# An fp32 transformer kernel on one core: another order of products in a pair of panels, and ScalarE's follow-up work an entry later

## The chip, the core and the metric

The kernel runs on one core of a Trainium2 chip. It is written instruction by instruction, with one program for each engine and semaphores between them: TensorE (PE, matmul), VectorE (DVE), ScalarE (ACT), GpSimd (POOL) and SyncE (SP, which only starts loads). The metric is the device time of one execution in microseconds (us).

## What is computed

Two transformer blocks over 256 tokens of width 2048, in fp32. Cut to what matters here:

```
# block 1
proj = rmsnorm(x) @ w_in ; da = diff_attention(...) ; ret = retention(...) * silu(rg)
x = x + concat(da, ret) @ w_o
hx = rmsnorm(x) ; hm = rmsnorm(mem)
xq, xk, xv = hx @ w_xq, hm @ w_xk, hm @ w_xv
x = x + attention(xq, xk, xv) @ w_xo
hf = rmsnorm(x)
x = rmsnorm(x + (silu(hf @ w_gate) * (hf @ w_up)) @ w_down)
# block 2
h = rmsnorm(x) * (1 + scale) + shift          # shift, scale, gate = silu(c) @ w_ada + b_ada
q, k, v, gate_a, u, gate_p = split(h @ w_in_2)
y_a = windowed_gqa(q, k, v) * silu(gate_a) ; y_p = multiscale_pool(u) * silu(gate_p)
g_a, g_p = split(sigmoid(h @ w_merge + b_merge))
merged = g_a * (y_a @ w_branch_attn) + g_p * (y_p @ w_branch_pool)
out = x + gate * rmsnorm(merged @ w_out)
```

Nearly all of the arithmetic is the product of 256 tokens with weight matrices, and all weights are read once.

## The kernel before

**Splitting.** PE multiplies fp32r operands, which carry fewer bits than fp32. So each operand is split into a high and a low part, and each product becomes three matmuls: high by high, low by high, high by low (the lines L1015, L1016, L1017; `ah`, `al`, `bh`, `bl`, `fah` and so on are the activations' parts, `whi` and `wlo` those of the weights).

**Halves and entries.** The weights come as halves of 256 rows by 512 columns (512 KB, one DMA each, in 8 slots `raw`). A *panel* is 512 output columns over all rows: 4 chunks of two halves for most, its two token tiles of 128 tokens (tile 0 and tile 1) in two PSUM banks `ps`. For each *entry* of the stream (840 of them) ACT makes the high part `whi` (L1524) and DVE the low part `wlo` (L2222, high part subtracted from `raw`), into one of 4 buffers; PE then takes the entry in one *step*. A normal step is 12 matmuls (both tiles). While PE is at step k, ACT and DVE may make entry k+3, and that of k+4 only when step k is done.

**Pairs.** 40 pairs of panels (q0 to q39; a first panel f and a second panel s) save work by Strassen's scheme in the Winograd form on their first chunk: seven *products* M1 to M7 of one tile and six matmuls each, in place of eight. Their weights are the four halves of the first chunks or sums of them; their activations are the plain forms or combined ones (`fah`, `fal`, `fbh`, `fbl`). M5, M6, M7 and M4 take sums of halves: DVE makes such a sum in the raw slot (L2238), and it waits there for its own conversion before (it overwrites what that read). The dictionary `sums_before` says ahead of which entry's conversion each sum is made. A product's result has to reach up to two banks: ACT copies a bank to `side` (L1122, `snapshot`: s5 of M5, s1 of M1, s3 of M7; the bank belongs to the other panel until then), and DVE makes the difference "v" (L1647, `difference`), for which M7 waits. The order of a pair with 4 chunks before is M3, M5, n1, M1, M2, n2, M6, n3, n4, M7, n5, M4, n6, ..., where n1, n2, ... are normal entries of f, counted as entries 0 to 12: n1 is entry 2, M1 is 3, M2 is 4, M6 is 6, n3 is 7, M7 is 9, M4 is 11. In this numbering snapshot s5 is taken at n1's step, whose tile 1 needs M5's bank back, s1 at M2's, the difference at n3's, s3 at n5's.

**What follows a panel.** When a panel ends, each engine runs a `begin(p)` for its kind: `o`, `xo`, `d`, `e`, `m` are added to X or to a tensor (`residual`, L1724; `merge_gate`, DVE L2054 and ACT L1396), `g`, `rg`, `ga`, `gp` get a sigmoid on ACT (L1174) and a product on DVE (`gate_product`), `u` is DVE's `up` (L1926 and L1929). ACT squares X for the norms (`square`, L1046; `residual_squares`). Where that work is a generator, `jobs.start` puts it in a queue of which one piece is run in each step; `aside.start` puts it in a second queue, whose next piece is run in each step, right after that step's `make`, the conversion of one more entry. A plain call in `begin` runs at once, ahead of the next conversion. The second panel of a pair has its tile-1 result whole in its PSUM bank and its tile-0 result split over bank and `side`, so DVE adds both first (`summed`, L1625).

**Names used here.** The kinds of panels in order: v, tq, rg (block 1's w_in), o, xk, xv, xq, xo, then g, u (gate, up) and d, e (down, the last down panels), then block 2's q, ga, pu, gp, kv, m (merge), ba, bp, w_out. q6 is o2/o3, q7 xk0/xk1, q14 xo2/xo3, q15 g0/u0, q16 g1/u1, q33 pu0/gp0. The residual of a pair's second panel is taken at the start of the pair behind it.

## Time and profile before

| | |
|---|---|
| median of 3 runs | 2186.24 us (2186.16 to 2189.12) |
| the profiled execution | 2193.24 us, its span 2191.4 us |
| PE busy | 2095.8 us, 96% of the span |
| DVE busy | 1681.4 us, 77% |
| ACT busy | 1172.8 us, 54% |
| granted clock of PE, mean | 0.989 of full |
| moved by DMA | 453.75 MB, 207 GB/s |

Busy PE is an upper bound on useful PE: matmuls are pipelined, and the profile models their ends. A main matmul lasts 390 ns by the profile but the next starts 0.227 us after it where nothing holds it, so what the profile calls idle is about 0.17 us less than the gap that a wait makes from start to start. Times of one place come from one execution, the profiled one.

### The profile page before, as it was taken

How to read it: one execution, taken by the hardware profiler on the slowest of the kernel's cores; microseconds unless marked ns; L12 is line 12 of the kernel's file. 1: busy time of each engine (PE TensorE's matmuls, PEld its weight loads, DVE VectorE, ACT ScalarE, POOL GpSimd, SP SyncE). 2: the span in 40 equal slices, each digit the busy share in tenths (PEclk: the TensorE clock that was granted, in tenths of full speed). 3: DMA queues.
4: the chain of work that ended last, by engine and by line, in shares of the span. 5: the costliest groups of instructions: out<-in, count | busy, mean ns of one | idle time of the engine just before them, and what ended most of it. 6: DMA issues, size and time to landing. Idle time of an engine off the chain costs nothing.

```text
span 2191.4 us, 25376 instructions
## 1 busy us (share of the span) xinstructions
PE 2095.8 (96%) x9334; PEld 1707.6 (78%) x9334; DVE 1681.4 (77%) x1839; ACT 1172.8 (54%) x1519; POOL 72.1 (3%) x94
## 2 busy tenths in 40 slices
PE   9999999899999999999999999999899999899998
PEld 7877787688887777787778877887677787678786
DVE  6767777776765678888888888887687767788875
ACT  6555555655554565554455544555655554554453
POOL 1000000000000000000000000000400000000000
PEclk9999999999999999999999999999999999999999
DMA  9444546466444447676567766665455556669653
GB/s 329 154 154 168 171 165 223 161 213 220 154 154 154 154 154 277 242 275 247 211 221 255 279 224 225 237 250 189 141 189 173 173 183 216 225 227 356 230 203 108
DMA packets 218955, 453.75 MB, mean 207 GB/s; under 512 B 14400, under 2 KB 16592, under 8 KB 218704
## 3 DMA queue, kind: packets, MB, share of 16 engines
q1 hardware_dynamic: 212928, 432.07, 56.0%
q0 software_dynamic: 5616, 19.94, 2.7%
q8 instruction: 74, 1.21, 0.2%
q14 instruction: 49, 0.40, 0.1%
q10 hardware_dynamic: 288, 0.13, 0.0%
HBM read 447.88 MB, written 4.19 MB: 206 GB/s over the span
## 4 chain that ended last, share of the span: by engine, by line
PE 52%; DVE 20%; issue 11%; DMA 11%; ACT 6%; SPq 0%; POOL 0%; DVEq 0%; ACTq 0%; POOLq 0%
PE ps L1015 16%; PE ps L1017 15%; PE ps L1016 15%; DVE wlo L2222 9%; DMA raw<-in_w_up_dram 3%; ACT whi L1524 3%; DVE raw L2238 3%; DMA raw<-in_w_down_dram 3%; PE ps L607 1%; DMA raw<-in_w_gate_dram 1%; DMA raw<-in_w_o_dram 1%; DVE FR L1889 1%; DMA raw<-in_w_merge_dram 1%; DMA raw<-in_w_in_dram 1%; DVE FR L1625 1%
## 5 line engine op out<-in xcount | busy, mean ns | idle before, releaser
L2222 DVE TENSOR_TENSOR wlo<-raw,whi 128x1024 fp32r<-128x1024 f32 x832 | 1005.7, 1221 | 323.6 <-ACT whi L1524 318.0
L1524 ACT ACTIVATE whi<-raw 128x1024 fp32r<-128x1024 f32 x840 | 880.0, 1056 | 624.4 <-PE ps L1017 372.1
L1015 PE MATMUL ps<-whi,ah 128*128 128x512 f32 x1618 | 650.6, 402 | 33.2 <-ACT side L1122 17.2
L1017 PE MATMUL ps<-whi,al 128*128 128x512 f32 x1618 | 634.3, 392 | 0.0
L1016 PE MATMUL ps<-wlo,ah 128*128 128x512 f32 x1618 | 633.9, 392 | 0.0
L1015 PEld LDWEIGHTS ps<-whi,ah 128*128 128x128 f32 x1618 | 306.1, 189 | 108.7 <-ACT side L1122 21.0
L1015 PE MATMUL ps<-whi,bh 128*128 128x512 f32 x862 | 345.8, 401 | 18.5 <-ACT side L1122 12.4
L1017 PEld LDWEIGHTS ps<-whi,al 128*128 128x128 f32 x1618 | 306.0, 189 | 66.1
L1016 PEld LDWEIGHTS ps<-wlo,ah 128*128 128x128 f32 x1618 | 306.5, 189 | 60.5 <-issue 0.2
L1017 PE MATMUL ps<-whi,bl 128*128 128x512 f32 x862 | 338.2, 392 | 0.0
L1016 PE MATMUL ps<-wlo,bh 128*128 128x512 f32 x862 | 337.9, 392 | 0.0
L2238 DVE TENSOR_TENSOR raw<-raw 128x1024 f32<-128x1024 f32 x160 | 195.9, 1224 | 45.3 <-DVE wlo L2222 24.2
L1015 PEld LDWEIGHTS ps<-whi,bh 128*128 128x128 f32 x862 | 163.5, 190 | 58.4 <-ACT side L1122 14.3
L1017 PEld LDWEIGHTS ps<-whi,bl 128*128 128x128 f32 x862 | 163.1, 189 | 35.1
L1016 PEld LDWEIGHTS ps<-wlo,bh 128*128 128x128 f32 x862 | 163.5, 190 | 33.2 <-issue 1.0
L1889 DVE SCALAR_TENSOR_TENSOR FR<-raw,Z,FR 128x1024 f32<-128x1024 f32 x90 | 111.5, 1279 | 0.9 <-DMA raw<-in_w_ada_dram 0.9
L1015 PE MATMUL ps<-whi,fah 128*128 128x512 f32 x208 | 85.0, 408 | 9.0 <-DVE wlo L2222 4.2
L1122 ACT ACTIVATE side<-ps 128x512 f32<-128x512 f32 x120 | 71.1, 592 | 32.1 <-PE ps L1017 31.9
L1017 PE MATMUL ps<-whi,fal 128*128 128x512 f32 x208 | 81.9, 394 | 0.0
L1016 PE MATMUL ps<-wlo,fah 128*128 128x512 f32 x208 | 81.6, 392 | 0.0
L2280 POOL TENSOR_TENSOR Z<-Z 128x2 f32<-128x2 f32 (+1 forms) x18 | 11.7, 655 | 1556.9 <-DVE Z L1570 854.2
L1625 DVE TENSOR_TENSOR FR<-ps,side 128x512 f32<-128x512 f32 x81 | 53.3, 686 | 8.5 <-PE ps L1017 8.3
(235 smaller groups left out, 1346.3 us busy)
## 6 DMA issues: line engine op xcount, KB each, us to landing
raw<-in_w_in_dram SPq DMA_DIRECT2D x168, 512.0 KB, 5.6
raw<-in_w_ada_dram SPq DMA_DIRECT2D x96, 512.0 KB, 8.0
raw<-in_w_gate_dram SPq DMA_DIRECT2D x88, 512.0 KB, 7.6
raw<-in_w_up_dram SPq DMA_DIRECT2D x88, 512.0 KB, 6.5
raw<-in_w_down_dram SPq DMA_DIRECT2D x88, 512.0 KB, 7.7
raw<-in_w_merge_dram SPq DMA_DIRECT2D x64, 512.0 KB, 6.6
raw<-in_w_o_dram SPq DMA_DIRECT2D x32, 512.0 KB, 8.0
raw<-in_w_xk_dram SPq DMA_DIRECT2D x32, 512.0 KB, 6.3
```

The lines of the kernel that those rows point to most:

```text
L607: ins = e.transpose(T[b].ap[:, kk * 256 + t * 128:kk * 256 + t * 128 + 128], src[:, t, (2 * b + kk) * 128:(2 * b + kk + 1) * 128], ident[: ...
L1015: e.matmul(o, xh[:, k, tokens], wh, start=first, stop=False, skip_group_check=more)
L1016: e.matmul(o, xh[:, k, tokens], wl, start=False, stop=False, skip_group_check=more)
L1017: ins = e.matmul(o, xl[:, k, tokens], wh, start=False, skip_group_check=more, stop=kk == 1 and (st.end or st.form in READ))
L1122: done(e.activation(side_of(pair[place[0]], place[1]), bank_of(pair[panel], t)[:, :], ACT.Copy), "snap")
L1524: done(e.activation(whi[:, n % HALVES, :], raw[:, item % RAWS, :], ACT.Copy), "hi")
L1625: return e.tensor_tensor(dst, src, side_of(p, t), side_op(p))
L1889: done(e.scalar_tensor_tensor(acc, src, csilu[:, k:k + 1], acc, ALU.mult, ALU.add), "ada")
L2222: done(e.tensor_tensor(wlo[:, n % HALVES, :], src, whi[:, n % HALVES, :].bitcast(F32), ALU.subtract), "lo")
L2238: done(e.tensor_tensor(place(item), place(add), place(item), ALU.subtract if minus else ALU.add), "t_sum")
L2280: e.tensor_tensor(dst, src, mhalf[:, 0:n], ALU.pow).then_inc(s["r"], 1)
```

## The change

In a pair of 4 chunks the order becomes M3, M5, n1, M1, n2, M6, M2, n3, n4, M7, ...: n2 is entry 4, M6 is 5, M2 is 6. Snapshot s1 is taken at n2's step, the difference v at M2's (entry 6). DVE makes M6's sum ahead of entry 1's conversion instead of entry 2's, M7's ahead of entry 5's instead of 4's. A pair of 3 chunks keeps its order of entries. On ACT the squares behind `o` and `xo` panels, the merge gates and the squares of the last down panels go through `aside`, and so run one conversion later; on DVE the means that need the squares do. For second panels DVE's additions and gate products and ACT's sigmoids of gates take tile 1 first; the merge gates' sigmoids on ACT still take tile 0 first. In `up` tile 1's product comes first, then the sum of tile 0 and its product, with nothing between these two.

ACT behind the end of panel o3, that is in the first steps of q7. `sq2` are the squares of the X of o3, `ev10` and `ev11` DVE's additions of o panels' results, `pre` the matmul side of a snapshot; before:

```order
L1524 ACTIVATE whi<-raw 128x1024 [waits s_half,s_raw4]
L1258 ACTIVATE bh<-FR,G 128x256 [waits s_half,s_mt_t2]
L1258 ACTIVATE bh<-FR,G 128x256 x3
L1046 ACTIVATE junk,Z<-X 128x512 [waits s_sq2,s_ev11,s_ev10]
L1046 ACTIVATE junk,Z<-X 128x512 [waits s_sq2]
L1524 ACTIVATE whi<-raw 128x1024 [waits s_half,s_raw2]
L1524 ACTIVATE whi<-raw 128x1024 [waits s_half,s_raw3]
L1122 ACTIVATE side<-ps 128x512 [waits s_pre,s_half]
L1524 ACTIVATE whi<-raw 128x1024 [waits s_half,s_raw5]
```

and in the changed kernel:

```order
L1535 ACTIVATE whi<-raw 128x1024 [waits s_half,s_raw4]
L1267 ACTIVATE bh<-FR,G 128x256 [waits s_half,s_mt_t2]
L1267 ACTIVATE bh<-FR,G 128x256 x3
L1535 ACTIVATE whi<-raw 128x1024 [waits s_half,s_raw2]
L1054 ACTIVATE junk,Z<-X 128x512 [waits s_sq2,s_ev11,s_ev10]
L1054 ACTIVATE junk,Z<-X 128x512 [waits s_sq2]
L1535 ACTIVATE whi<-raw 128x1024 [waits s_half,s_raw5]
L1130 ACTIVATE side<-ps 128x512 [waits s_pre,s_half]
L1535 ACTIVATE whi<-raw 128x1024 [waits s_half,s_t_sum]
```

The two squares (L1046, now L1054) have moved behind the conversion that followed them, and one conversion instead of two lies between them and the snapshot (L1122, now L1130).

DVE from M5's sum of pair q16 on, with the `up` of u0 in it (L2238 are sums, L2222 conversions, L1625 the sum of tile 0, L1926 and L1929 the products); before:

```order
L2238 TENSOR_TENSOR raw<-raw 128x1024 [waits s_lo,s_t_sum,s_raw6,s_raw5]
L2222 TENSOR_TENSOR wlo<-raw,whi 128x1024 [waits s_hi] x2
L2238 TENSOR_TENSOR raw<-raw 128x1024 [waits s_lo,s_t_sum,s_raw5,s_raw4]
L2222 TENSOR_TENSOR wlo<-raw,whi 128x1024 [waits s_hi]
L1625 TENSOR_TENSOR FR<-ps,side 128x512 [waits s_snap,s_half]
L1926 SCALAR_TENSOR_TENSOR FR<-ps,Z,FR 128x512 [waits s_gated]
L1929 SCALAR_TENSOR_TENSOR FR<-FR,Z 128x512 [waits s_ev10]
L2222 TENSOR_TENSOR wlo<-raw,whi 128x1024 [waits s_hi]
L2238 TENSOR_TENSOR raw<-raw 128x1024 [waits s_lo,s_t_sum,s_raw4,s_raw6]
L2222 TENSOR_TENSOR wlo<-raw,whi 128x1024 [waits s_hi] x3
L2238 TENSOR_TENSOR raw<-raw 128x1024 [waits s_lo,s_t_sum,s_raw4,s_raw7]
L2222 TENSOR_TENSOR wlo<-raw,whi 128x1024 [waits s_hi]
```

and in the changed kernel (L2257, L2241, L1643, L1944 and L1948 in this order):

```order
L2257 TENSOR_TENSOR raw<-raw 128x1024 [waits s_lo,s_t_sum,s_raw6,s_raw5]
L2241 TENSOR_TENSOR wlo<-raw,whi 128x1024 [waits s_hi]
L2257 TENSOR_TENSOR raw<-raw 128x1024 [waits s_lo,s_t_sum,s_raw5,s_raw4]
L2241 TENSOR_TENSOR wlo<-raw,whi 128x1024 [waits s_hi] x2
L1944 SCALAR_TENSOR_TENSOR FR<-ps,Z,FR 128x512 [waits s_gated,s_half]
L1643 TENSOR_TENSOR FR<-ps,side 128x512 [waits s_snap,s_half]
L1948 SCALAR_TENSOR_TENSOR FR<-FR,Z 128x512 [waits s_ev10]
L2241 TENSOR_TENSOR wlo<-raw,whi 128x1024 [waits s_hi] x2
L2257 TENSOR_TENSOR raw<-raw 128x1024 [waits s_lo,s_t_sum,s_raw4,s_raw6]
L2241 TENSOR_TENSOR wlo<-raw,whi 128x1024 [waits s_hi] x2
L2257 TENSOR_TENSOR raw<-raw 128x1024 [waits s_lo,s_t_sum,s_raw4,s_raw7]
L2241 TENSOR_TENSOR wlo<-raw,whi 128x1024 [waits s_hi]
```

M6's sum (the second L2238) is one conversion earlier, M7's (the third) one later; the product of tile 1 stands ahead of the sum of tile 0.

DVE further on in the same pair, up to the difference for M7 (L1647, now L1665); before:

```order
L1616 TENSOR_TENSOR FR<-FR 128x2x128 [waits s_dve]
L2222 TENSOR_TENSOR wlo<-raw,whi 128x1024 [waits s_hi]
L1620 TENSOR_TENSOR fbl<-FR,fbh 128x1024 [waits s_f_hi]
L2222 TENSOR_TENSOR wlo<-raw,whi 128x1024 [waits s_hi]
L1647 TENSOR_TENSOR side<-ps,side 128x512 [waits s_snap,s_half]
L2222 TENSOR_TENSOR wlo<-raw,whi 128x1024 [waits s_hi] x5
```

and in the changed kernel:

```order
L1634 TENSOR_TENSOR FR<-FR 128x2x128 [waits s_dve]
L2241 TENSOR_TENSOR wlo<-raw,whi 128x1024 [waits s_hi]
L1665 TENSOR_TENSOR side<-ps,side 128x512 [waits s_snap,s_half]
L1638 TENSOR_TENSOR fbl<-FR,fbh 128x1024 [waits s_f_hi]
L2241 TENSOR_TENSOR wlo<-raw,whi 128x1024 [waits s_hi] x6
```

The difference now stands ahead of the low part of the combined form (L1620, now L1638) and of one more conversion.

The diff (without the empty parts of its context):

```diff
--- before.py
+++ after.py
@@ -334,13 +334,16 @@
         product("M5", b12, b11, start=True, job=False)
         normal(f, *next(todo), snap=("s5", q))
         product("M1", b11, start=True, job=False)
-        product("M2", b21, start=True, snap=("s1", q))
         if chunks == 4:
+            normal(f, *next(todo), snap=("s1", q))
+            product("M6", b22, b12)
+            product("M2", b21, start=True, snap=("v", q))
             normal(f, *next(todo))
-        product("M6", b22, b12)
-        normal(f, *next(todo), snap=("v", q))
-        if chunks == 4:
             normal(f, *next(todo))
+        else:
+            product("M2", b21, start=True, snap=("s1", q))
+            product("M6", b22, b12)
+            normal(f, *next(todo), snap=("v", q))
         product("M7", b11, b22, minus=True)
         normal(f, *next(todo), snap=("s3", q))
         product("M4", b21, b22, aside=q)
@@ -446,6 +449,11 @@
 
         def side_op(p):
             return ALU.add if role[p][0] else ALU.subtract
+
+        def by_bank(p):
+
+
+            return (1, 0) if role.get(p, (0, 0))[0] else (0, 1)
 
         def nth_of(kinds, paired):
 
@@ -1165,7 +1173,7 @@
                         e.wait_ge(*gate_done(gate_before(p), t))
                 if root is not None:
                     e.wait_ge(s["r"], root_n(root))
-                for t in range(2):
+                for t in by_bank(p):
                     by = 1.0 if root is None else root_col[root][:, t:t + 1]
                     src = bank_of(p, t)[:, :]
                     if side_of(p, t) is not None:
@@ -1249,6 +1257,7 @@
                 wait_panel(p)
                 for t in range(2):
                     square(X[:, t, j * PW:(j + 1) * PW], ss[:, 2 * j + t:2 * j + t + 1], name)
+                yield
 
             def split_mem(j):
                 hi, _ = hi_lo(("mem", j))
@@ -1297,12 +1306,13 @@
 
             def down2(p, j):
                 for t in range(2):
-                    c = 4 * t + j
-                    xs = X[:, t, j * PW:(j + 1) * PW]
                     e.wait_ge(*ev(p, t))
-                    square(xs, ssf[:, c:c + 1], "sqf")
+                    square(X[:, t, j * PW:(j + 1) * PW], ssf[:, 4 * t + j:4 * t + j + 1], "sqf")
+                yield
+                for t in range(2):
                     e.wait_ge(s["gf_x"], 2 * j + t + 1)
-                    square(xs, ssg[:, c:c + 1], "sqg")
+                    square(X[:, t, j * PW:(j + 1) * PW], ssg[:, 4 * t + j:4 * t + j + 1], "sqg")
+                yield
 
             def scale_chunk(j, t):
                 e.wait_ge(s["r"], root_n(f"rr{t}"))
@@ -1394,6 +1404,7 @@
                 for t in range(2):
                     e.wait_ge(*ev(p, t))
                     done(e.activation(SIG[i][:, t, :], SIG[i][:, t, :], ACT.Sigmoid), "mg_sig")
+                yield
 
             def turn_merged(n):
                 yield
@@ -1437,7 +1448,7 @@
                     aside.start(sigmoids(p, GR, SG, "x"))
                     jobs.start(ret_pair(i))
                 elif kind == "o":
-                    residual_squares(p, i, ss_2, "sq2")
+                    aside.start(residual_squares(p, i, ss_2, "sq2"))
                     if i < 3:
                         jobs.start(turn_x(f"hx{i}", ("hx", i), gcols("nx", i)))
                     if i == 0:
@@ -1453,7 +1464,7 @@
                     if i == 0:
                         jobs.start(make_forms("xo"))
                 elif kind == "xo":
-                    residual_squares(p, i, ss_3, "sq3")
+                    aside.start(residual_squares(p, i, ss_3, "sq3"))
                     jobs.start(turn_x(f"hf{i}", ("hf", i), gcols("nffn", i)))
                     if i == 0:
                         jobs.start(make_forms("hf"))
@@ -1466,7 +1477,7 @@
                     if i % 4 == 0:
                         jobs.start(make_forms(f"h{i}"))
                 elif kind == "e" and i < 3:
-                    down2(p, i)
+                    aside.start(down2(p, i))
                 elif kind == "e":
                     last_down(p, t)
                 elif kind == "kv":
@@ -1481,7 +1492,7 @@
                     aside.start(sigmoids(p, GS[i], SG3, None))
                     jobs.start(pool_job(i))
                 elif kind == "m":
-                    merge_gate(p, i)
+                    aside.start(merge_gate(p, i))
                 elif kind == "ba" and i == 2:
                     jobs.start(pause(4))
                 elif kind == "bp":
@@ -1569,6 +1580,13 @@
                     after_own(done(e.tensor_reduce(src, given, AX_X, ALU.add)))
                 done(e.tensor_scalar(col, src, 1.0 / total, EPS, ALU.mult, ALU.add), "ms")
 
+            def mean_of(name, squares, ss):
+
+                yield
+                e.wait_ge(s[squares], 8)
+                mean(name, sums[name], 2, D, by_tile(ss))
+                yield
+
             def by_tile(ss):
                 return ss.rearrange("p (j t) -> p t j", t=2)
 
@@ -1696,7 +1714,7 @@
                 aside.start(gate_product(p, dst, sg, root))
 
             def gate_product(p, dst, sg, root):
-                for t in range(2):
+                for t in by_bank(p):
                     count["sig"] += 1
                     e.wait_ge(s["sig"], count["sig"])
                     src = bank_of(p, t)[:, :]
@@ -1719,7 +1737,7 @@
                 wait_sum(p, 1)
                 if p in role:
                     e.wait_ge(*side_taken(p, 1 - role[p][0]))
-                for t in range(2):
+                for t in by_bank(p):
                     xs = X[:, t, j * PW:(j + 1) * PW]
                     took(e.tensor_tensor(xs, bank_of(p, t)[:, :], xs, ALU.add), p, t)
 
@@ -1921,20 +1939,22 @@
                     yield
 
             def up(p, i):
-                summed(p, 0, HH[:, 0, :])
+                wait_sum(p, 1)
                 wait_gate(index["g", i], 0, 1)
                 took(e.scalar_tensor_tensor(HH[:, 1, :], bank_of(p, 1)[:, :], root_col["r3"][:, 1:2], ZG[:, 1, :],
                                             ALU.mult, ALU.mult), p, 1)
+                summed(p, 0, HH[:, 0, :])
                 e.wait_ge(*ev(p, 0))
                 done(e.scalar_tensor_tensor(HH[:, 0, :], HH[:, 0, :], root_col["r3"][:, 0:1], ZG[:, 0, :], ALU.mult,
                                             ALU.mult), "hh")
 
             def down2(p, j):
-                residual(p, j)
+                yield
                 for t in range(2):
                     xs = X[:, t, j * PW:(j + 1) * PW]
                     e.wait_ge(s["sqf"], 2 * j + t + 1)
                     done(e.tensor_tensor(xs, xs, GF[:, j * PW:(j + 1) * PW], ALU.mult), "gf_x")
+                yield
 
             def scale_chunk(j, t):
                 e.wait_ge(s["r"], root_n(f"rr{t}"))
@@ -2049,7 +2069,7 @@
             def merge_gate(p, i):
                 wait_sum(p, 1)
                 e.wait_ge(*side_taken(p, 1 - role[p][0]))
-                for t in range(2):
+                for t in by_bank(p):
                     also = BB[i] if side_of(p, t) is None else SIG[i][:, t, :]
                     took(e.tensor_tensor(SIG[i][:, t, :], bank_of(p, t)[:, :], also, ALU.add), p, t)
 
@@ -2117,8 +2137,7 @@
                 elif kind == "o":
                     residual(p, i)
                     if i == 3:
-                        e.wait_ge(s["sq2"], 8)
-                        mean("r2", sums["r2"], 2, D, by_tile(ss_2))
+                        aside.start(mean_of("r2", "sq2", ss_2))
                     else:
                         jobs.start(to_stationary(f"hx{i}", ("hx", i), gcols("nx", i)))
                     if i == 0:
@@ -2136,8 +2155,7 @@
                 elif kind == "xo":
                     residual(p, i)
                     if i == 3:
-                        e.wait_ge(s["sq3"], 8)
-                        mean("r3", sums["r3"], 2, D, by_tile(ss_3))
+                        aside.start(mean_of("r3", "sq3", ss_3))
                     jobs.start(to_stationary(f"hf{i}", ("hf", i), gcols("nffn", i)))
                     if i == 0:
                         jobs.start(make_forms("hf"))
@@ -2155,7 +2173,8 @@
                 elif kind == "e" and i < 3:
                     if i == 0:
                         e.wait_ge(s["norm_f"], 16)
-                    down2(p, i)
+                    residual(p, i)
+                    aside.start(down2(p, i))
                 elif kind == "e":
                     last_down(p, t)
                 elif kind == "kv":
@@ -2240,7 +2259,8 @@
 
             sums_before = {}
             for _, at in stream.pairs:
-                sums_before |= {at["M3"]: at["M5"], at["M5"] + 1: at["M6"], at["M2"]: at["M7"], at["M6"] + 1: at["M4"]}
+                sums_before |= {at["M3"]: at["M5"], at["M5"]: at["M6"], at["M1"] + 2: at["M7"],
+                                max(at["M2"], at["M6"]) + 1: at["M4"]}
 
             done(e.memset(tbl[:, :], 0.0), "tbl_zero")
             e.wait_ge(s["tbl_zero"], 1)
```

A `yield` ends a piece of such work; the next piece runs in the next step.

## Rows read from the trace of the kernel before

**Rows 1.** The page: busy time of the engines, and the chain that ended last

```profile
PE 2095.8 (96%) x9334; PEld 1707.6 (78%) x9334; DVE 1681.4 (77%) x1839; ACT 1172.8 (54%) x1519; POOL 72.1 (3%) x94
PE 52%; DVE 20%; issue 11%; DMA 11%; ACT 6%; SPq 0%; POOL 0%; DVEq 0%; ACTq 0%; POOLq 0%
```

**Rows 2.** Waits of PE: engine, tile, line, releaser: us in total, times, longest us

```profile
PE ps L1015 <- ACT side L1122: 29.6, 13, 5.0
PE ps L1015 <- DVE wlo L2222: 27.0, 31, 2.3
PE ps L1015 <- DVE side L1647: 7.3, 6, 1.9
```

**Rows 3.** Timeline of ACT, pair q14: start, duration, line, operation, [idle before <-releaser]

```profile
763.72 0.63 ACT L1046 ACTIVATE junk<-X 128x512 bf16<-128x512 f32 x1 [5.20 <-DVE X L1724]
765.10 1.99 ACT L1524 ACTIVATE whi<-raw 128x1024 fp32r<-128x1024 f32 x2
766.99 0.58 ACT L1122 ACTIVATE side<-ps 128x512 f32<-128x512 f32 x1
767.47 1.05 ACT L1524 ACTIVATE whi<-raw 128x1024 fp32r<-128x1024 f32 x1
```

**Rows 4.** Timeline of PE, the waits on s5 in q7, q14 and q15

```profile
417.38 0.79 PE L1015 MATMUL ps<-whi,bh 128*128 128x512 f32 x1 [5.01 <-ACT side L1122]
767.62 0.57 PE L1015 MATMUL ps<-whi,bh 128*128 128x512 f32 x1 [3.48 <-ACT side L1122]
814.93 0.50 PE L1015 MATMUL ps<-whi,ah 128*128 128x512 f32 x1 [1.24 <-ACT side L1122]
```

**Rows 5.** Timeline of DVE and PE, the merge gate of q36

```profile
1861.63 1.28 DVE L2054 TENSOR_TENSOR FR<-ps,FR 128x512 f32<-128x512 f32 x2
1866.01 0.50 PE L1015 MATMUL ps<-whi,ah 128*128 128x512 f32 x1 [2.58 <-ACT side L1122]
```

**Rows 6.** Timeline of ACT and PE, the gate of q33

```profile
1700.67 0.63 ACT L1174 ACTIVATE FR<-FR 128x512 f32<-128x512 f32 x1
1703.27 0.50 PE L1015 MATMUL ps<-whi,ah 128*128 128x512 f32 x1 [1.21 <-ACT side L1122]
```

**Rows 7.** Timeline of DVE in q16, and the page's group of its sums

```profile
853.76 2.44 DVE L2222 TENSOR_TENSOR wlo<-raw,whi 128x1024 fp32r<-128x1024 f32 x2
856.40 1.23 DVE L2238 TENSOR_TENSOR raw<-raw 128x1024 f32<-128x1024 f32 x1 [0.20 <-DVE wlo L2222]
874.32 1.23 DVE L1620 TENSOR_TENSOR fbl<-FR,fbh 128x1024 fp32r<-128x1024 f32 x1
L2238 DVE TENSOR_TENSOR raw<-raw 128x1024 f32<-128x1024 f32 x160 | 195.9, 1224 | 45.3 <-DVE wlo L2222 24.2
```

**Rows 8.** Timeline of PE, the waits on the difference in q7 and q16

```profile
436.27 0.47 PE L1015 MATMUL ps<-whi,fbh 128*128 128x512 f32 x1 [1.86 <-DVE side L1647]
877.43 0.47 PE L1015 MATMUL ps<-whi,fah 128*128 128x512 f32 x1 [1.36 <-DVE side L1647]
```

**Rows 9.** Stretches: us, busy time of PE, PEld, DVE, ACT, POOL, PEclk, DMA share, GB/s

```profile
437.00:440.50 3.50, 3.50 (x12) 2.77 (x12) 3.02 (x7) 2.15 (x5) 0.72 (x1) 0.54 0.41 102
1867.00:1870.40 3.40, 3.40 (x9) 2.64 (x9) 3.40 (x4) 1.06 (x1) 0.00 (x0) 0.50 0.00 0
1963.90:1967.40 3.50, 3.50 (x16) 2.85 (x17) 3.50 (x4) 2.37 (x4) 0.00 (x0) 1.00 0.03 9
1006.00:1036.00 30.00, 28.80 (x127) 23.19 (x125) 23.91 (x24) 11.49 (x12) 0.00 (x0) 1.00 0.91 334
```

**Rows 10.** Timeline of PE, waits on low parts in q16 (two), q20 and e2

```profile
858.81 0.50 PE L1015 MATMUL ps<-whi,ah 128*128 128x512 f32 x1 [0.77 <-DVE wlo L2222]
864.43 0.50 PE L1015 MATMUL ps<-whi,ah 128*128 128x512 f32 x1 [0.76 <-DVE wlo L2222]
1036.66 0.50 PE L1015 MATMUL ps<-whi,fbh 128*128 128x512 f32 x1 [1.86 <-DVE wlo L2222]
1547.65 0.50 PE L1015 MATMUL ps<-whi,bh 128*128 128x512 f32 x1 [0.73 <-DVE wlo L2222]
```

## The prediction, made before the changed kernel had run

> **What bounds the kernel now.** I read the page first: TensorE (PE) is busy 96% of the span, VectorE (DVE) 77%, and the chain that ended last is PE for 52% of the span and DVE for 20% [rows 1]. So what can be won is PE's idle time, and most of the chain's DVE part lies where DVE's preparation of a weight half reaches PE just in time. Then the waits of PE: three kinds stand out, and the change touches all three [rows 2]. (1) 29.6 us in 13 waits on ScalarE's (ACT) copy of M5's bank, the snapshot; by the kernel's order this is tile 1 of the first normal entry of a pair. (2) 27.0 us in 31 waits on a low part. (3) 7.3 us in 6 waits on the difference that M7 needs. The time of one such wait, its pair (q0 to q39, in the order of the program) and its entry come from PE's timeline, where I counted matmuls: a normal entry has twelve, a product six. My sum goes against the profiled execution's own time, 2193.24 us (span 2191.4); it is 7.0 above the median of the runs, 2186.24, so I take the gain off that median.
>
> **The change part by part.**
>
> *ACT work an entry later.* In the pair o2/o3, after the residual of the panel before, ACT stood idle 5.20 us for X, ran the two squares (763.72 to 765.10), two conversions of high parts (1.99 us), and only then the snapshot at 766.99 [rows 3]; PE stood 3.48 us for it [rows 4]. The change puts one of these two conversions ahead of the squares, into the idle time; the order shows it, one conversion left between the squares and the snapshot. The second of two conversions adds 1.99 − 1.05 = 0.94, say 0.95 us, to the first in these rows, so the snapshot comes 0.95 earlier. Nothing else holds it: M5 ended long before. This holds in four pairs, q6, q7, q14 and q15, whose waits are all longer than 0.95 (the last is 1.24 [rows 4]): −3.8. The cost, that squares come later, falls on DVE's mean of them, which is put off as well. What the whole wait holds beyond that stays, since the squares still block the queue ahead of the snapshot.
>
> *Merge gates (m panels, q36 to q38).* The same move: −0.95. But DVE now adds tile 1 first and ACT's sigmoid still asks for tile 0 first. DVE's two additions take 1.28 together [rows 5], so the second ends some 0.60 after the first, and the sigmoids start 0.60 later: −0.35 each, −1.05 for three waits of 2.58. *The sigmoid in q33* takes tile 1 from PSUM first, and no longer waits for DVE's sum ahead of it; one activation of 0.63 leaves the path of a wait of 1.21 [rows 6]: −0.65.
>
> *M7's wait.* The difference moves from the seventh step of a pair to the sixth, so DVE makes it ahead of one conversion (and, in the feed-forward panels, of the 1.23 us low part of the forms) instead of behind. That is 1.14 to 2.3 us earlier by the lengths of these operations [rows 7]. It covers q3's 0.3 and q7's 1.86 [rows 8]: −2.2. Behind q7's wait the clock granted to PE is 0.54 of full for 3.5 us [rows 9], that is 1.2 GHz in place of 2.4 for nearly all of it. It costs 3.5 × 0.46 = 1.6 us at most. If the wait is gone I take this window to be gone, less a little: −1.4. Against it: which waits bring such a window isn't plain from the rows. Behind q36's wait of 2.58, at 1866.01, there was one (0.50), behind q38's equally long one at 1963.75 none (1.00) [rows 5, 9].
>
> *Feed-forward pairs q16 to q29.* There DVE is just in time. M2's low part is late in nine pairs, 6.0 us together by PE's timeline, of which q16's 0.76 is typical [rows 10]; by start to start each is 0.17 more: 7.5. M7's difference is late in three, 1.36 in q16 [rows 8], 3.8 together, with 0.17 each 4.3. The change puts M7's sum behind the conversion of the half at entry 4, which frees a sum there: 1.14 + 0.20 of wait = 1.35, more than any of these stalls; M6's sum goes ahead of M5's low part. So 11.8 could go. Off it come three costs. First, the up panels: DVE multiplies tile 1 first, sums tile 0, and must then wait for its own result. Where DVE waits for itself now, ahead of a sum, it stands 0.20 us [rows 7]. 11 × 0.20 = 2.2. Second, M6's sum ahead of M5's low part: in q16 the conversion ran 853.76 to 856.20, PE took M5 at 856.5, a slack of 0.3, so M5 comes 1.35 − 0.3 = 1.05 late; but the first normal entry behind it already waited 0.77 (0.94 start to start) for the low part behind that sum [rows 7, 10], and that one doesn't move. Net +0.15, in eight pairs 1.2. Third, part of it comes back at the next pair's M3 in q20, q21, q26 and q27, whose first conversion hangs on loads that come in a burst (the DMA share is 0.91 over 30 us ahead of q20's wait of 1.86) [rows 9, 10]: 1.0. In all −11.8 + 2.2 + 1.2 + 1.0 = −7.4. The bounds: −11.8, and 0 if all comes back at M3.
>
> On the up panels a rule speaks against my cost. The Trainium skill, "VectorE: DVE Perf Modes", section "The DRAIN you can't avoid", says that eight copies with a semaphore after each take as long as eight with one at the end, the semaphore costs nothing extra. By it the self-waits are free and the sum would be 2.2 better. The trace doesn't agree: two operations of DVE without a wait between them overlap by 0.08 (the pair of conversions takes 2.44 for twice 1.22), those that wait for the one before start 0.20 after its end [rows 7]. I keep 2.2.
>
> *The rest.* q31's M2 0.5. Down panels e0 to e2 (the last ones, ahead of the final norm): the squares leave the way of the conversions behind them, whose lateness PE saw twice, 0.73 [rows 10] and 0.52 in the panel before: −1.25. M6 now stands ahead of M2, and its bank or side may wait for M1's snapshot where ACT is busy (q2, q32, q33): +0.6, between 0 and 3 × 0.58, a snapshot's length [rows 3]. Loads: halves are released in the order of the new entries, no more and no fewer; M2 and M6 swap two raw slots a microsecond or two: 0, hidden behind queues that run a pair ahead outside the feed-forward, and inside counted in the third cost.
>
> Sum: −3.8 − 1.05 − 0.65 − 2.2 − 1.4 − 7.4 − 0.5 − 1.25 + 0.6 = −17.65. The profiled execution would be 2175.6, the median 2168.6. I say 2169.
>
> **The rivals.**
> *A, the feed-forward gain is given back.* The stretch from a pair's last products to the next M3 is paced by loads (DMA share 0.91 [rows 9]); then what M2 and M7 win is waited for at M3 or the first normal entry. Against it: only four of 14 pairs have a wait at M3, and the burst is started by DVE's conversions, which come earlier too. The 7.4 and the e panels' 1.25 are gone: −9.0, 2177.
> *B, more low-clock windows go.* Waits of 3.48, 5.01, 3.48 and 2.58 [rows 4, 5] shrink to about 2.5, 4.1, 2.5 and 2.2. If q6, q14, q36 and q37 lose theirs, four times 1.5 come on top: −23.7, 2162.5. For it: the 2.58 at 1963.75 that went without a window; against it: the 2.58 at 1866.01 that didn't [rows 9].
> *C, slower: M6's sum ahead of M5's low part throws every feed-forward pair back.* The price is s per pair at M5, up to 1.35, if the wait of the first normal entry isn't relieved in turn. In 14 pairs 18.9 less the 2.3 relieved in q16, q21 and q26, plus the up panels' 2.2, against −9.25 for what lies outside these pairs: +9.6, 2196. It decides from s = (9.25 + 2.3 − 2.2)/14 = 0.67 on. Against it: in q16 the slack leaves 1.05 and 0.94 of it is relieved [rows 7, 10].
> *D, ACT's moves do nothing*, since the snapshot's start is set by X and not by what stands between. Then −4.85 and half the clock are missing: −12, 2174. This lies in the forecast's range.
>
> **How the numbers follow.** Forecast with D 0.56, A 0.20, B 0.17, C 0.07. The likeliest alone: 2164 to 2174. The range holds A and B, and leaves out C and the outer ends: 2158 (B with the feed-forward's 11.8 instead of 7.4) to 2181 (A without the clock, the merges and half of the squares). No change, within 0.2% (4.4 us, about what a measurement can tell here), needs A to lose the squares' part as well, or a mild C: 0.08. Slower by more: C's stronger half and what I haven't seen: 0.07. Faster 0.85.
>
> **What would show it.** The 13 waits on the snapshot fall from 29.6 to about 25; the six on the difference nearly vanish; in q16 the wait at entry 4 is gone, and one of about 1.0 stands at M5 in place of that at the first normal entry; ACT's idle ahead of the squares falls by 1 each; DVE's sum of tile 0 in the up panels is followed by 0.20 of waiting. Sigmoids of q36 to q38 start 0.6 later than X's first addition ends. I am wrong if waits at M3 grow by as much as those at M2 shrink (A), if new waits at M5 are not matched by vanished ones (C), or if waits appear at M6 for M1's snapshot in more than three pairs.

## The result, and the profile after

| | before | changed |
|---|---|---|
| median of the runs | 2187.68 us (4 runs, 2186.16 to 2189.51) | 2174.6 us (4 runs, 2171.12 to 2177.47) |
| ratio of the runs | | 0.9939, 95% interval 0.992 to 0.9958 |
| the profiled execution | 2193.24 us | 2175.93 us |
| its span, mean granted clock | 2191.4 us, 0.989 | 2174.1 us, 0.993 |

The changed kernel is 13.1 us faster by the medians (0.6%), 17.3 us by the profiled executions. Forecast was 17.65 for both. The profiled execution came to 2175.93 us (2175.6 was forecast); the median, 2174.6, lies in the stated range of 2158 to 2181, 5.6 above the 2169 and just outside the likeliest stretch of 2164 to 2174. (One of the eleven executions of e2 below took 4645.87 us; its ratio leaves that one out, and its median is 2188.3 us without it and 2188.4 with it.) The page after, its busy times and the chain that ended last, against [rows 1]:

```profile
PE 2085.0 (96%) x9334; PEld 1700.7 (78%) x9334; DVE 1681.1 (77%) x1839; ACT 1173.4 (54%) x1519; POOL 74.2 (3%) x94
PE 57%; DVE 19%; issue 11%; DMA 8%; ACT 5%; POOL 0%; DVEq 0%; ACTq 0%; SPq 0%; POOLq 0%
```

No engine has less work; PE's busy time falls by 10.8 mostly because it runs less at the low clock. The waits of PE after, against [rows 2] (other lines between these are left out):

```profile
PE ps L1023 <- ACT side L1130: 24.6, 17, 4.0
PE ps L1023 <- DVE wlo L2241: 24.3, 29, 2.2
PE ps L756 <- DVE FR L1877: 1.5, 1, 1.5
PE ps L615 <- issue: 2.0, 2, 1.2
PE ps L788 <- DVE Z L1917: 2.1, 1, 2.1
PE ps L1023 <- DVE side L1665: 1.5, 1, 1.5
```

The snapshot's waits have lost 5.0 us but there are 17 instead of 13. The 13 that were there alone fell by 8.2, to 21.4; four new ones (M6 in q2, q32 and q33, M4 in q7) hold 3.2. Those on the difference fell from 7.3 to 1.5; those on low parts from 27.0 to 24.3 only; and three kinds have come (L615, L756, L788) that are PE's own jobs: its transposes and small products between the steps. (A job's piece is run behind a step, and PE waits there for what other engines make of the piece before.)

**Where the time lies.** I cut all traces at the start of each pair's M3. The granted clock falls to 0.5 of full (1.2 GHz instead of 2.4) in single stretches, most of them 3.4 us long, called low windows here. PE takes twice as long for the same work in one, so of each pair's length I took off half of the time at a granted clock of 0.5 within it (47.8 us in all before, 29.7 after). What is left, less that of the kernel before, in us:

| pairs | changed | e1 | e2 | e3 | f3 | f4 |
|---|---|---|---|---|---|---|
| q0 to q5 | +1.2 | +0.6 | +1.2 | −1.4 | −1.6 | −1.7 |
| q6, q7, q14, q15 | −3.8 | −5.8 | +0.8 | −6.9 | −12.1 | −12.5 |
| q12, q13 | +1.9 | −1.8 | +1.8 | +0.4 | +0.6 | +0.6 |
| q16 to q29 (feed-forward) | −4.7 | +2.5 | −6.3 | −4.8 | −4.2 | −5.5 |
| q30 and the e panels | −0.6 | −1.4 | −0.4 | −0.6 | −0.6 | −0.6 |
| q31 to q34 | +1.0 | −0.8 | +1.5 | +2.4 | +2.4 | +2.3 |
| q35 to q38 (merges) | −1.5 | −1.2 | −0.1 | −3.5 | −3.8 | −9.0 |
| rest | −1.8 | −1.8 | −0.5 | −0.9 | +0.3 | −0.3 |
| all | −8.3 | −9.6 | −2.0 | −15.3 | −19.0 | −26.7 |
| at the low clock, us | 29.7 | 35.9 | 51.5 | 25.4 | 16.6 | 11.5 |

(The columns are the experiments below, each from its one profiled execution; the rest holds the start, q8 to q11 and q39. A group repeats within about 1.5 us where nothing was changed, or 2 where a low window falls into a stretch with waits: the −1.8 of e1 at q12 is such a one.) So of the 17.35 us between the spans 8.3 are work and waiting, 9.05 are low-clock time. This split is not exact: before, q20 and q27 held one low window each, and in e1, which has the same order there, both went without a window and took as long (46.17 and 44.18 us, before 45.81 and 44.17). There PE waits for loads and low parts anyway, so these two windows cost nothing. Put so, work is −11.7 and the clock −5.6. Nor is all of the clock's part the change's doing. Besides the windows of q20 and q27, that behind q7's M7, half of the long one behind q7's snapshot and those of q36 and q37 went, 6.8 us in time together. Windows also went ahead of q0, in q1 and in q30, and others came in q2, q12 and q38; these six cancel, and a longer stretch in q39 costs 1.15. The window ahead of q0, where none of the moved work runs, is there in some of the versions and not in others. And the kernel before is here by its profiled execution, 5.6 us above its median, so a part of the differences in the traces isn't in the medians.

**ScalarE in q14**, to be read against [rows 3] (start, duration, line, operation, idle before it):

```profile
757.87 1.06 ACT L1535 ACTIVATE whi<-raw 128x1024 fp32r<-128x1024 f32 x1 [1.66 <-PE ps L1025]
760.97 0.63 ACT L1054 ACTIVATE junk<-X 128x512 bf16<-128x512 f32 x1 [2.04 <-DVE X L1742]
762.36 1.04 ACT L1535 ACTIVATE whi<-raw 128x1024 fp32r<-128x1024 f32 x1
763.30 0.57 ACT L1130 ACTIVATE side<-ps 128x512 f32<-128x512 f32 x1
```

The conversion at 757.87 now stands in the idle time ahead of the squares (5.20 has become 1.66 + 2.04), and the snapshot starts 2.33 us after the start of the squares, where it was 3.27: 0.94 earlier, as worked out. PE's waits on it in q7, q14 and q15, against [rows 4]:

```profile
412.91 0.50 PE L1023 MATMUL ps<-whi,bh 128*128 128x512 f32 x1 [4.01 <-ACT side L1130]
763.93 0.50 PE L1023 MATMUL ps<-whi,bh 128*128 128x512 f32 x1 [2.08 <-ACT side L1130]
810.21 0.50 PE L1023 MATMUL ps<-whi,ah 128*128 128x512 f32 x1 [0.24 <-ACT side L1130]
```

They were 5.01, 3.48 and 1.24: −1.00, −1.40, −1.00; q6's went from 3.48 to 2.46. At the start of the same entry PE's wait for the low part fell too, in q7 from 2.27 to 1.14 and in q6 from 0.66 to 0.23.

**VectorE and PE in q16**, against [rows 7, 10]; first DVE from M6's sum on, then PE at M5:

```profile
850.43 1.22 DVE L2257 TENSOR_TENSOR raw<-raw 128x1024 f32<-128x1024 f32 x1 [0.20 <-DVE wlo L2241]
851.58 2.35 DVE L2241 TENSOR_TENSOR wlo<-raw,whi 128x1024 fp32r<-128x1024 f32 x2
853.85 0.74 DVE L1944 SCALAR_TENSOR_TENSOR FR<-ps,Z,FR 128x512 f32<-128x512 f32 x1
854.51 0.68 DVE L1643 TENSOR_TENSOR FR<-ps,side 128x512 f32<-128x512 f32 x1
855.22 0.75 DVE L1948 SCALAR_TENSOR_TENSOR FR<-FR,Z 128x512 f32<-128x512 f32 x1
855.89 2.35 DVE L2241 TENSOR_TENSOR wlo<-raw,whi 128x1024 fp32r<-128x1024 f32 x2
```

```profile
852.85 0.50 PE L1023 MATMUL ps<-whi,fah 128*128 128x512 f32 x1 [0.90 <-DVE wlo L2241]
```

The sum stands ahead of M5's conversion, PE waits 0.90 (1.07 start to start) at M5, the first normal entry waits no more, and neither does M2. In `up` the third operation starts 0.71 after the second, where it was 0.66 before: the self-wait costs 0.05 here, and the three together 0.12, not 0.20.

**PE's own jobs in q4**: the transposes (L615) of what comes of the products L715 to L717. After:

```profile
269.20 0.59 PE L717 MATMUL ps<-FR 128*128 128x256 f32 x2
273.74 0.63 PE L615 MATMUL ps<-ident,FR 128*128 128x128 f32 x4 [1.18 <-issue]
```

and before:

```profile
271.15 0.59 PE L709 MATMUL ps<-FR 128*128 128x256 f32 x2
275.71 0.61 PE L607 MATMUL ps<-ident,FR 128*128 128x128 f32 x4
```

The distance is the same (4.54 and 4.56): it is what ACT, GpSimd and DVE need in between (squares, a root, a product). Before, PE had n2 and M6 to do in between, 2.72 and 1.36 us (12 and 6 matmuls at 0.227); now it has M6 and M2, twice 1.36, and stands 1.18 us. In q13 it is the same with a single step: the piece that waits was behind n2 and is now behind M6. Before, then after:

```profile
723.43 0.55 PE L748 MATMUL ps<-ident,FR 128*128 128x128 f32 x3 [0.17 <-DVE FR L1859]
```

```profile
721.10 0.66 PE L756 MATMUL ps<-ident,FR 128*128 128x128 f32 x4 [1.52 <-DVE FR L1877]
```

The piece ahead of it starts 6.51 us earlier in both traces (716.92 and 714.59).

### The profile page after: what moved, and what is told of

The parts are those of the page before. It is cut to its first block, busy times and chain, and to the rows that moved or that the text cites. A ratio compares the mean times of both kernels' runs of the same rounds, so it can differ in the third digit from the quotient of the medians.

```text
span 2174.1 us, 25372 instructions
## 1 busy us (share of the span) xinstructions
PE 2085.0 (96%) x9334; PEld 1700.7 (78%) x9334; DVE 1681.1 (77%) x1839; ACT 1173.4 (54%) x1519; POOL 74.2 (3%) x94
## 3 DMA queue, kind: packets, MB, share of 16 engines
q8 instruction: 74, 1.21, 0.2%
## 4 chain that ended last, share of the span: by engine, by line
PE 57%; DVE 19%; issue 11%; DMA 8%; ACT 5%; POOL 0%; DVEq 0%; ACTq 0%; SPq 0%; POOLq 0%
PE ps L1023 17%; PE ps L1025 17%; PE ps L1024 17%; DVE wlo L2241 8%; DVE raw L2257 3%; DMA raw<-in_w_down_dram 3%; DMA raw<-in_w_up_dram 2%; ACT whi L1535 2%; PE ps L615 1%; DMA raw<-in_w_merge_dram 1%; DMA raw<-in_w_o_dram 1%; DVE FR L1907 1%; DVE FR L1643 1%; DMA raw<-in_w_gate_dram 1%; PE ps L746 1%
## 5 line engine op out<-in xcount | busy, mean ns | idle before, releaser
L2241 DVE TENSOR_TENSOR wlo<-raw,whi 128x1024 fp32r<-128x1024 f32 x832 | 1005.4, 1221 | 307.0 <-ACT whi L1535 300.7
L2257 DVE TENSOR_TENSOR raw<-raw 128x1024 f32<-128x1024 f32 x160 | 195.9, 1225 | 47.2 <-DVE wlo L2241 25.2
L1130 ACT ACTIVATE side<-ps 128x512 f32<-128x512 f32 x120 | 71.1, 592 | 29.9 <-PE ps L1025 29.9
L1023 PEld LDWEIGHTS ps<-whi,fah 128*128 128x128 f32 x208 | 39.1, 188 | 32.7 <-DVE wlo L2241 20.4
```

The lines of the kernel that those rows point to most:

```text
L1023: e.matmul(o, xh[:, k, tokens], wh, start=first, stop=False, skip_group_check=more)
L1130: done(e.activation(side_of(pair[place[0]], place[1]), bank_of(pair[panel], t)[:, :], ACT.Copy), "snap")
L2241: done(e.tensor_tensor(wlo[:, n % HALVES, :], src, whi[:, n % HALVES, :].bitcast(F32), ALU.subtract), "lo")
L2257: done(e.tensor_tensor(place(item), place(add), place(item), ALU.subtract if minus else ALU.add), "t_sum")
```

## The experiments

Each kernel ran beside the kernel before on the same chip. The times are medians, the ratios go against the kernel before. The changed kernel, the e's, the f's and the g's stand in four groups, on different chips, beside which the kernel before had medians of 2187.68, 2188.8, 2190.41 and 2188.34 us: a difference of two medians across groups is uncertain by some 2 us.

**e1: the follow-up work alone.** The changed kernel with the lines of `_pair` and `sums_before` as they were:

```diff
-            normal(f, *next(todo), snap=("s1", q))
-            product("M6", b22, b12)
-            product("M2", b21, start=True, snap=("v", q))
+        product("M2", b21, start=True, snap=("s1", q))
+        ...
-                sums_before |= {at["M3"]: at["M5"], at["M5"]: at["M6"], at["M1"] + 2: at["M7"],
+                sums_before |= {at["M3"]: at["M5"], at["M5"] + 1: at["M6"], at["M2"]: at["M7"], at["M6"] + 1: at["M4"]}
```

> The follow-up work of the change (ACT through aside, tile 1 first, up's order, means put off) with the old order of the pair and the old places of the sums. My account of the two traces gives this half nearly all of the gain that does not hang on low-clock windows: the waits on the snapshot in q6, q7, q14, q15, q33 and q36 to q38 shrink as in the changed kernel, M5 and M6 get no new waits, PE's own jobs stay where they were. So about -9 us against the kernel before, 2178 to 2180. Rival (the order is the better half): -5 or less, and the new waits at M3 are there too.

Measured: 2178.31 us, ratio 0.9955 (0.9942 to 0.9967), before 2188.8. That is 10.5 us of the changed kernel's 13, and the intervals of the two ratios overlap. The waits of PE on the snapshot and the rest in its trace:

```profile
PE ps L1020 <- DVE wlo L2238: 27.6, 30, 1.7
PE ps L1020 <- ACT side L1127: 23.6, 13, 4.0
PE ps L1020 <- DVE side L1662: 6.8, 6, 1.5
```

13 waits on the snapshot again, 6.0 us less in them; the low parts as before, and the difference 0.5 less (q7's fell from 1.86 to 0.92). My account holds.

**e2: the order and the sums' places alone.** The reverse: only the diff's parts on `_pair` and `sums_before`, in the kernel before.

> The new order of a pair and the new places of the sums alone. My account: the waits at M2 and of M7 go (-12 with the start-to-start part), but eleven waits of about 0.9 appear at M5 in place of nine at the first normal entry, and PE's own jobs come up too early in q4, q5, q13 and q28 (+1.2, +0.8, +1.5, +2.1), M6 waits for M1's snapshot in three pairs (+2.2): -1 to -4 against before, 2183 to 2187. Rival (the order is the better half, jobs don't matter): -8 or more.

Measured: 2188.36 us, ratio 0.9998 (0.9988 to 1.0009). Nothing. Its waits of PE (the third line, ahead of all pairs, isn't the order's doing: the kernel before waits 2.6 us there):

```profile
PE ps L1018 <- ACT side L1125: 30.7, 17, 5.0
PE ps L1018 <- DVE wlo L2225: 22.0, 29, 1.9
PE ps L610 <- DVE FR L1689: 2.4, 1, 2.4
PE ps L783 <- DVE Z L1902: 2.3, 1, 2.3
PE ps L741 <- issue: 2.3, 1, 2.3
PE ps L610 <- issue: 2.0, 2, 1.2
```

In the feed-forward the order does bring 6.3 (the table), and it loses it elsewhere: on the jobs, and at M6, where PE now waits for M1's snapshot in q2, q32 and q33 (0.67, 0.91, 0.67). By this one trace 2.0 us of work are won in all, and 51.5 us at the low clock instead of 47.8 take 1.85 back.

**e3: M2's step without a piece of the jobs.** In the changed kernel:

```diff
-            product("M2", b21, start=True, snap=("v", q))
+            product("M2", b21, start=True, snap=("v", q), job=False)
```

> The changed kernel, but M2's step of a pair of 4 chunks runs no piece of the jobs, so PE's own transposes and small products behind it come one step later. If the waits of PE in q4, q5, q13 and q28 come from two short products in a row (M6, M2) between two pieces of a job, they go: 1.2 + 0.8 + 1.3 + 2 = about 5 us better than the changed kernel, and the three waits at M6 in q2, q32, q33 stay. Rival: the waits only move to another step, or jobs run late elsewhere: no change or slower.

Measured: 2165.96 us, ratio 0.9894 (0.9881 to 0.9908), 8.6 us below the changed kernel's median. By pairs, against the changed kernel and with the clock taken out: q4 −1.4, q5 −0.8, q2 −0.8, q7 −2.3, q12 −1.5, q32 −0.8. The waits in q4 and q5 are gone, as expected; q13's and q28's stayed (+0.1, −0.4), against what I expected, and q33 lost 1.5, for its jobs now wait in other steps (1.88 at M6, 1.58 at M7). q13's piece stands behind M6, whose step keeps its piece of the jobs in this edit. PE in q4:

```profile
267.54 0.59 PE L717 MATMUL ps<-FR 128*128 128x256 f32 x2
273.47 0.60 PE L615 MATMUL ps<-ident,FR 128*128 128x128 f32 x4
```

5.93 us apart now, and no idle time.

**e4: M6's sum back by one conversion.**

```diff
-                sums_before |= {at["M3"]: at["M5"], at["M5"]: at["M6"], at["M1"] + 2: at["M7"],
+                sums_before |= {at["M3"]: at["M5"], at["M5"] + 1: at["M6"], at["M1"] + 2: at["M7"],
```

> The changed kernel with M6's sum back ahead of the conversion of entry 2. If my working of the swap is right (what M5 loses the first normal entry has back), the eleven waits at M5 go, nine or so of 0.7 to 0.8 come back at the first normal entry, and the time is 1 to 2 us better or the same. Rival C (the sum ahead of M5's low part costs about 1 us a pair): 8 to 10 us better than the changed kernel.

Measured: 2179.14 us, ratio 0.995 (0.9937 to 0.9962). Not better than the changed kernel (0.9939, 0.992 to 0.9958), and not told apart from it. Rival C, which would give 8 to 10 us back here, is out: the waits at M5 were no loss of their own. In q1 the early sum even helps: PE's wait on the snapshot was 3.06 before and is 1.93 in the changed kernel; with this edit the pair is 1.06 us longer again.

In q28 the early sum costs. There a piece of PE's jobs waits for VectorE's sums of columns (L1917). In the changed kernel M6's sum for q29 stands ahead of them, one conversion between; then PE:

```profile
1428.51 1.23 DVE L2257 TENSOR_TENSOR raw<-raw 128x1024 f32<-128x1024 f32 x1 [0.20 <-DVE wlo L2241]
1430.79 1.28 DVE L1917 TENSOR_REDUCE Z<-ps 128x4 f32<-128x512 f32 x2
1431.53 0.44 PE L788 MATMUL ps<-ident,FR 128*128 128x128 f32 x2 [2.12 <-DVE Z L1917]
```

and with e4's edit the sum comes behind them:

```profile
1424.40 1.28 DVE L1917 TENSOR_REDUCE Z<-ps 128x4 f32<-128x512 f32 x2
1425.60 1.21 DVE L2257 TENSOR_TENSOR raw<-raw 128x1024 f32<-128x1024 f32 x1
1425.14 0.44 PE L788 MATMUL ps<-ident,FR 128*128 128x128 f32 x2 [0.61 <-DVE Z L1917]
```

q28 is 1.8 us shorter for it, with the clock taken out, and q29, the pair behind, 1.1 longer.

**f1: the merge gates' sigmoids in VectorE's order.**

```diff
             def merge_gate(p, i):
-                for t in range(2):
+                for t in by_bank(p):
                     e.wait_ge(*ev(p, t))
```

> The changed kernel, with the merge gates' sigmoids on ScalarE in the order in which VectorE adds (tile 1 first). I priced the mismatch at 0.60 for each of q36 to q38: their waits on the snapshot of M5 fall from 1.93 to about 1.3, 1.8 in all; the total, 2173, can't be told from the changed kernel's by time alone. Rival: the sigmoids wait for something else than the first addition, and the waits stay 1.93.

Measured: 2171.46 us, ratio 0.9913 (0.9896 to 0.993). By time not told from the changed kernel. By PE's timeline the waits of q36 to q38 are 1.00, 0.75 and 1.41 instead of 1.93, 1.93 and 1.91: 2.6 us, somewhat more than the 1.8; those at M3 of the same pairs grew by 1.0 in turn, and two of the three at M5 are gone. Its time at the low clock is 43.7 us, against 29.7 in the changed kernel, with windows in q36 and q37 again although the waits there are shorter. The sigmoids, changed kernel first:

```profile
1844.52 2.01 ACT L1535 ACTIVATE whi<-raw 128x1024 fp32r<-128x1024 f32 x2 [0.33 <-DMA raw<-in_w_merge_dram]
1849.16 1.15 ACT L1406 ACTIVATE FR<-FR 128x512 f32<-128x512 f32 x2 [2.64 <-DVE FR L2074]
```

```profile
1847.03 2.00 ACT L1535 ACTIVATE whi<-raw 128x1024 fp32r<-128x1024 f32 x2 [0.34 <-DMA raw<-in_w_merge_dram]
1851.07 1.23 ACT L1406 ACTIVATE FR<-FR 128x512 f32<-128x512 f32 x2 [2.04 <-DVE FR L2074]
```

The idle time ahead of them is 2.64 and 2.04: the 0.60 of the prediction.

**f2: up as before.**

```diff
-                wait_sum(p, 1)
-                wait_gate(index["g", i], 0, 1)
+                summed(p, 0, HH[:, 0, :])
+                wait_gate(index["g", i], 0, 1)
...
-                summed(p, 0, HH[:, 0, :])
```

> The changed kernel, with VectorE's up as before (sum of tile 0, product of tile 1, product of tile 0). I priced the new order at 0.20 a panel; the changed kernel's trace rather shows 0.05 to 0.12 (the third operation starts 0.71 after the second instead of 0.66). With 0.20, 2.2 us better; with 0.1, 1 us; by a cost of nothing for the self-wait, the same. VectorE's three operations in q16 took 1.92 us up to the next conversion in the kernel before, 2.04 in the changed one: 1.92 expected here. Waits at M5 and M3 of the feed-forward pairs a little shorter.

Measured: 2177.72 us, ratio 0.9935 (0.9916 to 0.9955): the same as the changed kernel. In q16 the three operations and the conversion behind them take 1.92 (852.77 to 854.69) where the changed kernel has 2.04, and the feed-forward pairs together differ by 0.0 us. The 0.12 is real on DVE; in time, where 11 of them would be 1.3 us, it can't be seen.

```profile
852.77 0.69 DVE L1643 TENSOR_TENSOR FR<-ps,side 128x512 f32<-128x512 f32 x1
854.69 2.35 DVE L2240 TENSOR_TENSOR wlo<-raw,whi 128x1024 fp32r<-128x1024 f32 x2
```

**f3: the squares behind the snapshot.** e3, and

```diff
             def residual_squares(p, j, ss, name):
+                yield
+                yield
                 wait_panel(p)
...
             def mean_of(name, squares, ss):
                 yield
+                yield
+                yield
                 e.wait_ge(s[squares], 8)
```

> M2's step without a piece of the jobs (as in e3), and the squares behind o and xo panels two steps later still, behind M5's snapshot instead of ahead of it, the means that need them also two steps later. If the squares' wait for X is what holds the snapshot, the waits on M5's snapshot in q6, q7, q14 and q15 go (2.46 + 4.0 + 2.1 + 0.24, 8.8 us, and one or two low-clock windows): 2155 to 2158 against e3's 2166. Rival: VectorE, which adds X and converts after it, is late itself, so that PE waits for the low part of the first normal entry instead: half of it or less.

Measured: 2157.12 us, ratio 0.9847 (0.9832 to 0.9861), 8.8 below e3. By the traces, whose spans are 8.1 apart, the work of these four pairs is 5.2 less and the low clock costs 4.4 less (16.6 us of it after 25.4), while the other pairs have 1.5 more. ACT in q14, where the snapshot now waits for PE alone, 0.24 us, and the squares come after it:

```profile
745.03 1.06 ACT L1537 ACTIVATE whi<-raw 128x1024 fp32r<-128x1024 f32 x1 [0.30 <-PE ps L1025]
746.33 0.60 ACT L1130 ACTIVATE side<-ps 128x512 f32<-128x512 f32 x1 [0.24 <-PE ps L1025]
746.82 1.05 ACT L1537 ACTIVATE whi<-raw 128x1024 fp32r<-128x1024 f32 x1
747.77 0.62 ACT L1054 ACTIVATE junk<-X 128x512 bf16<-128x512 f32 x1
```

q6, q14 and q15 have no wait left at the first normal entry; in q7 PE waits at M1, M2 and further on instead (0.87, 0.73, 1.06, 1.11).

**f4: the merge gates' sigmoids behind the snapshot too,** in VectorE's order:

```diff
             def merge_gate(p, i):
-                for t in range(2):
+                yield
+                yield
+                for t in by_bank(p):
```

> As f3, and the merge gates' sigmoids also two steps later (behind M5's snapshot) and with tile 1 first. The waits of 1.93 in q36 to q38 go: 4 to 6 us better than f3, 2150 to 2153. Rival: waits move to the next snapshot (s1, for M6), then 1 us or nothing.

Measured: 2151.26 us, ratio 0.9819 (0.9805 to 0.9834). This is the best version: 1.8% below the kernel before, 23 us below the changed one. Its waits of PE:

```profile
PE ps L1023 <- DVE wlo L2247: 24.0, 27, 1.8
PE ps L1023 <- ACT side L1130: 9.9, 9, 1.9
```

The snapshot is down from 29.6 to 9.9 us; most of what is left waits for VectorE's low parts.

**g1: the order alone, and M2's step without a job.** e2 with e3's edit.

> The kernel before with the new order and sums alone (as e2, which measured no gain), and M2's step without a piece of the jobs. If the order's gain at M2 and M7 was really there in e2 and was eaten by PE's own jobs, it shows here: 6 to 8 us better than the kernel before, as e3 was 7 better than the changed kernel by the pairs' lengths. Rival: the order itself gives nothing (all of it back at M3 and M5), and e3's gain hangs on the follow-up work: 2 us or less.

Measured: 2181.01 us, ratio 0.9959 (0.9945 to 0.9972), 7.3 us below the kernel before. So the order was worth something in e2, and the piece of the jobs at M2's step took it. By the pairs, clock taken out, g1 is 5.6 us better than e2; most of that lies in q7 (3.1), q4, q12, q6, q5 and q2. q13's and q28's waits (1.53 and 1.94) are still there.

**g2: f4 with M6's sum back by one conversion,** e4's edit.

> The best kernel so far (f4), with M6's sum back ahead of the conversion of entry 2. By e4's trace against the changed kernel's, pair by pair, the sum's place moves the wait between M5 and the first normal entry and costs or gives 1 us at most: 2151 again, within 2. Rival C: the eleven waits of 0.9 at M5 were pure loss: 2142.

Measured: 2152.66 us, ratio 0.983 (0.9816 to 0.9844). The same as f4. By PE's timeline eleven waits of 0.65 to 0.91 at M5 (9.7 us) became eleven at the first normal entry (9.1 us, of which f4 had 1.0). q28's wait fell from 2.19 to 0.98, as in e4.

## Why the prediction was right, and where it was not

The direction, the range and roughly the size were right; the sum reached its size by luck, by errors against each other. The plainest of them is the split. By its terms the follow-up work gives 4.55 us (3.8 + 1.05 + 0.65 + 1.25, less the 2.2 of `up`) and the order with the sums 13.1. Measured alone, the follow-up work gave 10.5 (e1) and the order nothing (e2); in the traces e1's low clock costs 5.95 less than that of the kernel before. The median also fell on the number of rival D, 2174, whose mechanism is refuted. In the prediction's own terms:

- **ACT an entry later, −3.8.** Right: the four waits fell by 1.0, 1.0, 1.4 and 1.0, and e1 has them too, 1.0, 1.0, 1.1 and over 0.9. What had no term is the wait for the low part ahead of them in q6 and q7, which shrank by 0.4 and 1.1; e1's work in the four pairs is 5.8 less. *Merge gates −1.05, the gate of q33 −0.65.* 2.58 became 1.93, so −0.65 each and not −0.35, because M5's own wait takes a part (e1, without one, has 2.15 to 2.16); the 0.60 of mismatch was exact (f1). q33's wait fell from 1.21 to 0.52: −0.69.
- **M7's wait, −2.2.** The waits are gone in q3, q7 and the feed-forward. But in q7 0.63 and 0.96 us of waiting came behind it, at entry 10 for DVE's low part and at M4 for ACT's snapshot, and 1.11 at a job further on; q7 as a whole won 3.3 us in length, of which 3.4 is a shorter time at the low clock.
- **Feed-forward, −7.4.** Measured −4.7, or about −8 without crediting the two windows of q20 and q27. The parts: the waits at M2 and M7 went as worked out. M6's sum cost what I said in q16 (1.07 at M5 for 0.94 at the first normal entry). But I took the eight pairs with a late first normal entry from the trace of before; with M2 and M7 faster, the next pair starts sooner and has less in hand, so q17, q20, q23 and q27 wait at M5 too. In these 14 pairs seven waits at M5 (6.3 us) stand against three gone at the first normal entry (2.3), and those at M3 fell from 7.2 to 5.2, where I had them rise by 1.0. By start to start that is 2.9 for the 2.2 of the second and third cost: right in sum, for another reason. (Over the whole kernel the waits at M3 hold 8.8 us in 6 before and 9.3 in 9 after: what the feed-forward lost came in q36 to q38, 1.1 before and 3.6 after.) What I hadn't seen are two things. Behind M7, at entry 10 and elsewhere, DVE is late next: five waits, 1.6 us. And M6's early sum delays a job in q28 by 2.1 (e4). `up`'s 2.2 was too much: 0.12 a panel, and nothing that can be seen in time (f2). The 0.20 came from sums that wait for four semaphores; the product here waits for one. Whether that makes the difference wasn't tried. On the Trainium skill's rule ("VectorE: DVE Perf Modes", "The DRAIN you can't avoid": a semaphore after each operation costs nothing extra) the trace now has a number: the operation that waits for the one before it starts 0.03 after its end where the others overlap by 0.08, so in time here the rule is nearer than my 0.20.
- **M6 waits for M1's snapshot, +0.6.** It does in the three pairs named, 0.66, 0.91 and 0.67, 2.2 in all: undersized.
- **q31's M2, −0.5, and the down panels e0 to e2, −1.25.** q31 is 0.3 shorter: M2's wait of 0.64 went and one of 0.66 came at M5. PE's two waits in the e panels, 0.73 and 0.52, are gone in the changed kernel.
- **The step that failed: PE's own jobs, which have no term.** I counted what the order moves on DVE and ACT and not the pieces of jobs that go by steps: a short step in place of a long one brings a piece 1.4 us nearer to the one before it. It cost +1.4 in q4, +0.8 in q5 and +1.4 in q13, 3.6 us, and the piece at M2's step costs more in other pairs: taking it out gave 7 us by the pairs (e3; q7, q12, q2 and q32 besides q4 and q5) and 7.3 by the median (g1), where e2 measured nothing. q28's +2.2, which I expected to be the same (e2's and e3's expectation), isn't: there M6's early sum is what delays the job (e4, g2).
- **The clock, −1.4.** −9.05 by the records of this one execution (−5.6 where it counts), so the opposite error, 4 to 8 us. It is rival B in part, and chance in part, as said with the table: the windows behind q7's M7, q36 and q37 went, and the long one behind q7's snapshot is half as long; those behind q6 and q14 stayed, and q38, which had none behind 2.58 us of waiting, has one behind 1.91. What brings them stays open. The four runs of the changed kernel, 2171.12 to 2177.47, go with their granted clock, 0.995 to 0.992.

Rival D (ACT's moves do nothing) is refuted by e1, rival C by e4 and g2. Rival C's arithmetic has a slip too: the terms outside the feed-forward add up to 10.25, not 9.25, so it would have said 2195 instead of 2196 and decided from 0.74 on instead of 0.67. The sign about the snapshot came true by luck: the waits fell to 24.6 as said, "about 25", but as 21.4 in the old places and 3.2 in new ones.

What is open: what sets the waits at M3 in q20, q21, q26 and q27 (4.7 to 7.2 us together in the versions here). That loads in a burst do is argued from the DMA share of [rows 9] alone; it wasn't tried. For q13 the step that holds its piece is M6's, which e3 leaves as it is; taking that piece out wasn't tried.
